# Moving 16 modulation tiles of a layer trunk into its one-hot gates stage, with two product banks there and per-pair counts in the HGRN stage

## The chip, the cores and the metric

One core of one Trainium2 chip. The metric is the device time of one execution in microseconds (us); a stretch "from A to B" is counted from the start of the profiled span.

## What is computed

Two layers of a hybrid decoder trunk, for 256 prompt tokens and 8 x 4 sample tokens, model width 1024, all in float32. What matters here, cut from the reference:

```
mod = silu(c) @ w_ada + b_ada                 # c: 1 prompt row + 8 sample rows; w_ada: 1024 x 6144 a layer
sh1, sc1, gt1, sh2, sc2, gt2 = split(mod, 6)
h = rmsnorm(x, norm1) * (1 + sc1) + sh1       # before the input projection
oa = hgrn2(q, k, v, log_f, S0)                # per chunk: o = (q e^G) S + (masked q k decay) v
S  = S * e^Gl + (k e^(Gl - G))^T v            # the state that goes from chunk to chunk
x = x + gt1 * (mixer(h) @ w_out)
h = rmsnorm(x, norm2) * (1 + sc2) + sh2
x = x + gt2 * peer(h)                         # product-key experts: top 16 of 128 x 128 for 8 heads a token
```

`w_ada` is read as 48 tiles of 128 x 1024 a layer: six sections (the six names of the split) of eight tiles.

## The kernel before

**Stages.** `build` runs a loop over the two layers. In each, the blocks follow one another with a barrier of all engines between them: `project_block` (norm and input projection), `local_block` (RG-LRU and norms of the delta heads), `hgrn_block`, `delta_block`, `output_block`, `experts_block` (scores, top 16 and the first expert matrix), `gates_block` and `combine_block` (second expert matrix). All weights arrive as tiles of 512 KB; SyncE issues each load when the slot of a ring comes free (`ring`, three slots, and in the local and HGRN blocks `extra_ring`, four slots, in turn with it).

**The modulation tiles.** `SECTIONS` puts the two sections of the norm ahead of the input projection last, and they are those of the next layer, since that norm stands at a layer's start; `setup_block` computes the first layer's. A tile is one `ada_product` (line 509): four matmuls, each of 32 output rows by 256 columns, that add into the bank `ps_mod`. After eight tiles a section is complete: ScalarE copies the rows (`copy_rows`, line 532), TensorE turns them with two matmuls by the identity (`ada_turn`, line 517), and ScalarE copies the columns into `m.mod` (`copy_columns`, line 539). The next section may not start before that. In `local_block` 16 tiles and two turns run, in `hgrn_block` 32 tiles and four turns, put by hand between the block's own matmuls (`ada(first, end)` and `turn(n)` in its TensorE program). Bias and gain are applied in `delta_block` on VectorE (`add_bias`, `norm_gain`).

**`local_block` (line 846).** VectorE's chain ends with lines 971 and 972, which read the matmuls of line 903. Behind `turn(0)` TensorE has the second eight tiles and `turn(1)`, and ScalarE the two copies of that section.

**`hgrn_block` (line 975).** C = 8 positions a block, 32 blocks, two pairs of heads. VectorE makes for each distance d in 0 to 7 the products q*gate*key (`pairs`), TensorE sums them per head (`distance`, line 1116), VectorE multiplies by the values and adds (`values`, lines 1242 and 1243). GpSimd makes the decays (line 1095) and the decayed keys (`kt`, lines 1100 and 1102); `kt_ready` follows them, and TensorE waits for it before it transposes keys and values (lines 1138 and 1140), and only behind these comes `distance(2)`. ScalarE writes masked copies of the values (`mask_v`, line 1070) for four steps of eight blocks; two copies are held. A step's matmuls (line 1171) give the updates of eight blocks in `ps_outer`, and VectorE walks the state through the blocks, pair by pair (line 1270): 64 operations, each behind a wait for the one before (`link`, a `Chain`), also where the two pairs have nothing to do with each other. `read_states` (line 1150) reads the state of each block into `ps_sums`, after a whole step of the walk (`scan_ready`). The matmuls of the sample group (line 1195) come after the whole walk (`u_out` 8), then VectorE's lines 1279, 1280 and 1282.

**`gates_block` (line 2397).** 64 groups of four prompt tokens. For a group TensorE makes distances in `ps_d` (`spots`, line 2419), VectorE one-hot rows times gate weight (line 2472), GpSimd distances of the second key (line 2449), ScalarE a one-hot of these by Square and Relu (lines 2459 and 2461), TensorE four matmuls (line 2429) into one of four banks of `ps_g`, and VectorE multiplies the expert activations by them (line 2479). Each engine is held by counts: GpSimd and the one-hot rows of group q wait for the products of group q - 4 (`gate_ps`), the products of group q for both one-hots and for line 2479 of group q - 4. SyncE has nothing to do, and no DMA runs.

## Time and profile before

| | us |
|---|---|
| median of 3 runs | 2382.62 (2380.51 to 2385.88) |
| the profiled execution, its own time | 2376.54 |
| its span | 2374.7 |
| TensorE busy in the span | 2274.7 (96%) |
| VectorE | 1515.3 (64%) |
| ScalarE | 1264.8 (53%) |
| GpSimd | 1051.2 (44%) |

The profiled execution is 6.08 us under the median of the runs. "Busy" for TensorE takes in modelled ends of pipelined matmuls, so a busy TensorE isn't one at its peak. The mean granted TensorE clock is 0.968 of full speed.

### The profile page before, as it was taken

What the parts mean: (1) busy time and instruction counts of PE and PEld (TensorE: products, weight loads), DVE (VectorE), ACT (ScalarE), POOL (GpSimd) and SP (SyncE); (2) the same over time, 40 slices, a digit from 0 to 9 for tenths busy, and PEclk for the clock granted to TensorE, in tenths of its full rate; (3) what the DMA queues carried; (4) which work ended last, traced back from release to release, by engine and by line L of the source; (5) the groups of instructions that cost most, each with busy time, mean ns of one, the idle gap of its engine ahead of it and who ended that gap; (6) DMA issues with size and microseconds to landing.
All of it is one profiled execution on the core that took longest, in us unless ns stands there. A gap on an engine that the chain in (4) does not pass through costs nothing. (4 is left out here: it accounts for less than half of the span.)

```text
span 2374.7 us, 58407 instructions
## 1 busy us (share of the span) xinstructions
PE 2274.7 (96%) x20514; PEld 2085.6 (88%) x20514; DVE 1515.3 (64%) x3131; ACT 1264.8 (53%) x2431; POOL 1051.2 (44%) x960
## 2 busy tenths in 40 slices
PE   6978999999999999999999799999999999999998
PEld 4955869999998799999989367699999978999997
DVE  2747636963225968888656665299432278787885
ACT  2543315567557955555546322155665587555554
POOL 0001106884446746566300210088644475665661
PEclk7988999999999999999989789999999999999999
DMA  6466034556552079899544830455555512898992
GB/s 263 163 249 240 4 125 160 177 177 207 189 187 98 5 274 314 277 311 312 177 161 158 307 124 29 143 177 178 198 184 188 189 36 89 292 312 275 312 311 100
DMA packets 123806, 455.40 MB, mean 192 GB/s; under 512 B 13744, under 2 KB 14256, under 8 KB 122544
## 3 DMA queue, kind: packets, MB, share of 16 engines
q1 hardware_dynamic: 105264, 386.80, 45.7%
q0 software_dynamic: 18432, 67.12, 10.3%
q8 instruction: 72, 1.18, 0.2%
q14 instruction: 38, 0.31, 0.0%
HBM read 449.37 MB, written 4.49 MB: 191 GB/s over the span
## 5 line engine op out<-in xcount | busy, mean ns | idle before, releaser
L426 POOL TENSOR_TENSOR parts<-ring,parts 128x512 fp32r<-128x512 f32 x358 | 463.9, 1299 | 470.7 <-ACT parts L419 455.7
L419 ACT ACTIVATE parts<-ring 128x512 fp32r<-128x512 f32 x616 | 386.7, 631 | 359.5 <-PE ps_u L475 281.7
L471 PE MATMUL ps_u<-h_parts,parts 128*128 128x256 f32 x4096 | 563.6, 280 | 0.9 <-ACT parts L419 0.6
L2594 PE MATMUL ps_y<-act_parts,parts 128*128 128x256 f32 x4096 | 561.3, 279 | 0.0
L471 PEld LDWEIGHTS ps_u<-h_parts,parts 128*128 128x128 f32 x4096 | 514.6, 188 | 3.2 <-ACT parts L419 2.0
L2594 PEld LDWEIGHTS ps_y<-act_parts,parts 128*128 128x128 f32 x4096 | 513.6, 188 | 0.9 <-ACT parts L2534 0.7
L426 DVE TENSOR_TENSOR parts<-ring,parts 128x512 fp32r<-128x512 f32 x258 | 178.6, 695 | 382.1 <-ACT parts L419 359.3
L2643 POOL TENSOR_TENSOR act_parts<-big,act_parts 128x256 fp32r<-128x256 f32 x256 | 246.7, 964 | 302.2 <-ACT act_parts L2623 302.2
L475 PE MATMUL ps_u<-h_parts,parts 128*128 128x256 f32 x2048 | 322.8, 279 | 1.2 <-DVE parts L426 0.9
L2598 PE MATMUL ps_y<-act_parts,parts 128*128 128x256 f32 x2048 | 321.7, 279 | 0.0
L475 PEld LDWEIGHTS ps_u<-h_parts,parts 128*128 128x128 f32 x2048 | 275.4, 188 | 2.0 <-DVE parts L426 1.3
L2598 PEld LDWEIGHTS ps_y<-act_parts,parts 128*128 128x128 f32 x2048 | 274.8, 188 | 0.0
L2541 DVE TENSOR_TENSOR parts<-ring,parts 128x512 fp32r<-128x512 f32 x260 | 214.4, 846 | 74.6 <-ACT parts L2534 73.9
L2541 DVE TENSOR_TENSOR parts<-more_ring,parts 128x512 fp32r<-128x512 f32 x252 | 209.2, 850 | 73.0 <-ACT parts L2534 73.0
L2623 ACT ACTIVATE act_parts<-big 128x256 fp32r (+1 forms) x256 | 107.2, 419 | 219.8 <-PE ps_y L2598 213.7
L2534 ACT ACTIVATE parts<-ring 128x512 fp32r<-128x512 f32 x260 | 162.2, 625 | 49.4 <-PE ps_y L2598 49.4
L2534 ACT ACTIVATE parts<-more_ring 128x512 fp32r<-128x512 f32 x252 | 157.3, 624 | 45.3 <-PE ps_y L2598 45.3
L2429 PEld LDWEIGHTS ps_g<-onehot 128*128 128x128 f32 x1024 | 123.9, 191 | 40.6 <-issue 36.4
L2449 POOL TENSOR_TENSOR onehot<-keep,sel 128x512 f32<-128x512 f32 x128 | 132.7, 1039 | 36.7 <-PE ps_g L2429 27.6
L2429 PE MATMUL ps_g<-onehot 128*128 128x128 f32 x1024 | 144.5, 284 | 4.3 <-ACT onehot L2461 3.4
L471 PE MATMUL ps_z<-x_parts,parts 128*128 128x288 f32 x832 | 136.3, 305 | 1.6 <-ACT parts L419 1.6
L471 PEld LDWEIGHTS ps_z<-x_parts,parts 128*128 128x128 f32 x832 | 121.8, 196 | 2.0 <-ACT parts L419 2.0
(391 smaller groups left out, 2853.3 us busy)
## 6 DMA issues: line engine op xcount, KB each, us to landing
ring<-in_stream SPq DMA_DIRECT2D x522, 512.0 KB, 3.9
more_ring<-in_stream SPq DMA_DIRECT2D x126, 512.0 KB
extra_ring<-in_stream SPq DMA_DIRECT2D x48, 512.0 KB, 6.2
big<-in_stream SPq DMA_DIRECT2D x16, 512.0 KB, 11.6
out_state_out<-big SPq DMA_DIRECT2D x2, 1440.0 KB, 8.0
big<-in_state SPq DMA_DIRECT2D x2, 1280.0 KB, 11.3
big<-in_mixc SPq DMA_DIRECT2D x2, 1024.0 KB, 8.8
big<-in_spots SPq DMA_DIRECT2D x2, 1024.0 KB, 5.4
```

Of the source, the lines that this page charges most:

```text
L419: eng.activation(m.parts[:, q % PARTS, 0, :], half_tile(m, t, half), ACT.Copy).then_inc(s["hi_ready"], 1)
L426: eng.tensor_tensor(m.parts[:, q % PARTS, 1, :], half_tile(m, t, half), m.parts[:, q % PARTS, 0, :].bitcast(F32), ALU.subtract).then_inc(m ...
L471: pe.matmul(out, hi[:, k, :], hr[:, side, kk, 0:tokens], start=(kk + side == 0), stop=False)
L475: mm = pe.matmul(out, lo[:, k, :], hr[:, 0, kk, 0:tokens], start=False, stop=(kk == KD - 1))
L2429: mm = pe.matmul(ps_g[:, g % SETS, c, :], first[:, g % SETS, c, :], second[:, g % SETS, c, :], start=True, stop=True)
L2449: pool.tensor_tensor(second[:, g % SETS, :, :], spread(m.iota, 1, GROUP), spread(tokens_of(m.second_key, i, g), 2, P), ALU.subtract).then_ ...
L2534: act.activation(m.parts[:, q % PARTS, 0, :], tile[:, half * D // 2:(half + 1) * D // 2], ACT.Copy).then_inc(s["hi_ready"], 1)
L2541: v.tensor_tensor(m.parts[:, q % PARTS, 1, :], tile[:, half * D // 2:(half + 1) * D // 2], m.parts[:, q % PARTS, 0, :].bitcast(F32), ALU.s ...
L2594: pe.matmul(ps[:, half * KD // 2 + k, :], hi[:, k, :], act_parts[:, j % AHEAD, side, :], start=False, stop=False)
L2598: mm = pe.matmul(ps[:, half * KD // 2 + k, :], lo[:, k, :], act_parts[:, j % AHEAD, 0, :], start=False, stop=False)
L2623: act.activation(act_parts[:, j % AHEAD, 0, :], column(g, j), ACT.Copy).then_inc(s["act_hi"], 1)
L2643: pool.tensor_tensor(act_parts[:, j % AHEAD, 1, :], column(g, j), act_parts[:, j % AHEAD, 0, :].bitcast(F32), ALU.subtract).then_inc(s["ac ...
```

## The change

It takes the 16 tiles of the two last sections out of the local and HGRN blocks, of which each now has eight fewer (8 and 24; one turn and three). The gates block gets them: SyncE loads them into a ring of three slots of its own, TensorE runs one behind the products of groups 1, 4, 7, ... 22 and 33, 36, ... 54 and turns a section behind groups 26 and 58, ScalarE copies rows after its groups 23 and 55 and columns after 31 and 63, for which its one loop becomes four. `ps_d` has two banks in place of four, since `ps_next` needs one; `spots` runs two groups ahead in place of three; TensorE's loop over groups is written out. Bias and gain of these two sections go from the delta block into the combine block. In the HGRN block the state walk counts per pair (`after0`, `after1`) and each operation waits for its own pair's last one; `pairs` and `values` wait for the operations that they need; the samples' kept states are multiplied before the walk; the samples' matmuls run after three steps of the walk; TensorE's order is written anew. `parts` is allocated for the blocks that use it, to make room for the new ring.

```diff
-MODS_T = len(SECTIONS) * KD
-LOCAL_ADA = 16
+MODS_T = 4 * KD
+NEXT_T = len(SECTIONS) * KD - MODS_T
+LOCAL_ADA = 8
...
+T_NEXT = T_X + EXTRAS
+TILES = T_NEXT + NEXT_T
...
+    if i >= MODS_T:
+        return T_NEXT + i - MODS_T
...
             mm.then_inc(s["qk_spread"], 1)
             turn(0)
-            ada(KD, 2 * KD)
-            turn(1)
...
             copy_rows(act, m, s, rows, ps_mod, 0)
             copy_columns(act, m, s, ps_mod, 0, 1)
-            copy_rows(act, m, s, rows, ps_mod, 1)
-            copy_columns(act, m, s, ps_mod, 1, 2)
...
+            copy_rows(act, m, s, ada_rows, ps_mod, 1)
+            copy_columns(act, m, s, ps_mod, 1, 1)
...
-            copy_rows(act, m, s, ada_rows, ps_mod, 3)
-            copy_columns(act, m, s, ps_mod, 3, 2)
+            copy_rows(act, m, s, ada_rows, ps_mod, 2)
+            copy_columns(act, m, s, ps_mod, 2, 2)
             mask_v(2)
-            copy_rows(act, m, s, ada_rows, ps_mod, 4)
-            copy_columns(act, m, s, ps_mod, 4, 3)
             mask_v(3)
             mask_v(4)
-            act.wait_ge(s["scan_ready"], 4)
+            copy_rows(act, m, s, ada_rows, ps_mod, 3)
+            copy_columns(act, m, s, ps_mod, 3, 3)
+            for pair in range(A_PAIRS):
+                act.wait_ge(s[f"after{pair}"], BLOCKS)
             act.activation(m.states[:, 0:A_PAIRS, 0, :], after[:, :, BLOCKS - 1, :], ACT.Copy)
-            copy_rows(act, m, s, ada_rows, ps_mod, 5)
-            copy_columns(act, m, s, ps_mod, 5, 4)
...
-                        pe.wait_ge(s["cols_out"], i // KD - 2)
+                        pe.wait_ge(s["cols_out"], (i - LOCAL_ADA) // KD)
...
-            ada(16, 22)
+            ada(8, 14)
             distance(0)
             distance(1)
-            ada(22, 24)
+            ada(14, 16)
             turn(1)
-            ada(24, 26)
...
-                if d == 5:
+                if d == 6:
                     turn(2)
-                ada(*((26, 28), (28, 30), (30, 32), (32, 33), (33, 35), (35, 37))[d - 2])
+                ada(*((18, 20), (20, 21), (21, 22), (22, 24), (24, 25), (25, 26))[d - 2])
...
-                pe.wait_ge(s["scan_ready"], turn + 1)
-                for b in range(turn * TB // 2 + 1, min((turn + 1) * TB // 2 + 1, BLOCKS)):
+                for pair in range(A_PAIRS):
+                    pe.wait_ge(s[f"after{pair}"], HALF * (turn + 1))
+                for b in range(turn * HALF + 1, min((turn + 1) * HALF + 1, BLOCKS)):
...
+            def products(step):
                 pe.wait_ge(s["vm_ready"], step + 1)
                 for pair in range(A_PAIRS):
-                    n = 2 * step + pair
-                    if n >= 4:
-                        pe.wait_ge(s["u_out"], n - 3)
+                    if step >= 2:
+                        pe.wait_ge(s[f"after{pair}"], HALF * (step - 1))
                     for r in range(2):
...
                     mm.then_inc(s["u_ready"], 1)
-                if step == 1:
-                    turn(3)
-                    ada(40, 42)
-                if step == 0:
-                    pe.wait_ge(s["qt_ready"], 1)
-                    pe.wait_ge(s["values_done"], 1)
-                    for b in range(NB):
-                        for pair in range(A_PAIRS):
-                            for r in range(2):
-                                inter(pair, r, NP + NS * b, NS, m.state0[:, pair, b, :])
-                    ada(37, 40)
-                if step >= 2:
-                    read_states(step - 2)
-                    ada(38 + 2 * step, 40 + 2 * step)
-            ada(46, 48)
+
+            def sample_products():
+                pe.wait_ge(s["vm_ready"], 5)
+                for pair in range(A_PAIRS):
+                    pe.wait_ge(s[f"after{pair}"], HALF * 3)
+                    for r in range(2):
+                        rows = slice(r * HD, (r + 1) * HD)
+                        mm = pe.matmul(ps_outer[rows, pair, :], ktt[0:NB * NS, 2, pair, rows],
+                                       vm[0:NB * NS, 0, 2 * pair + r, :, :], start=True, stop=True)
+                    mm.then_inc(s["samples_u"], 1)
+
+            products(0)
+            products(1)
+            pe.wait_ge(s["qt_ready"], 1)
+            pe.wait_ge(s["values_done"], 1)
+            for b in range(NB):
+                for pair in range(A_PAIRS):
+                    for r in range(2):
+                        inter(pair, r, NP + NS * b, NS, m.state0[:, pair, b, :])
+            ada(26, 28)
+            products(2)
+            read_states(0)
+            products(3)
+            read_states(1)
+            ada(28, 32)
+            sample_products()
...
+            turn(3)
             mm = read_states(3)
             mm.then_inc(s["inter_ready"], 1)
-            turn(4)
...
+                dst = {k: compact((pair_s if k else pair_p)[:, d % 2, :], k, d) for k in kinds(d)}
+                if d == 0:
+                    for k in kinds(d):
+                        i = ve.tensor_tensor(dst[k], blocks(q, k, 0, length(k)), blocks(key, k, 0, length(k)), ALU.mult)
+                    i.then_inc(s["products_ready"], 1)
+                    return
+                decayed = {k: steps(ve.tensor_tensor(dst[k], blocks(q, k, d, length(k)), blocks(gate[d], k, d, length(k)),
+                                                     ALU.mult)) for k in kinds(d)}
+                for k in kinds(d):
+                    steps.wait(decayed[k])
+                    i = ve.tensor_tensor(dst[k], dst[k], blocks(key, k, 0, length(k) - d), ALU.mult)
...
+                    return
+                tmp, valued = {}, {}
+                for k in kinds(d):
+                    tmp[k] = compact(prod_s if k else prod_p, k, d)
+                    steps.wait(summed[k])
+                    valued[k] = steps(ve.tensor_tensor(tmp[k], a[k], blocks(v, k, 0, length(k) - d), ALU.mult))
+                for k in kinds(d):
+                    steps.wait(valued[k])
+                    summed[k] = steps(ve.tensor_tensor(blocks(o, k, d, length(k)), blocks(o, k, d, length(k)), tmp[k], ALU.add))
...
+            steps.wait(steps.n)
             ve.sem_inc(s["values_done"], 1)
+            ve.wait_ge(s["gates_ready"], 1)
+            for pair in range(A_PAIRS):
+                last = blocks(since, True, NS - 1, NS)[:, pair, :, :].broadcast_to([P, NB, HD])
+                kept = steps(ve.tensor_tensor(m.states[:, pair, 1:, :], m.state0[:, pair, :, :], last, ALU.mult))
...
+                            ve.wait_ge(s[f"after{pair}"], b)
...
-                        link(i)
-                ve.sem_inc(s["scan_ready"], 1)
-                ve.sem_inc(s["u_out"], 2)
-            ve.wait_ge(s["u_ready"], 9)
+                        i.then_inc(s[f"after{pair}"], 1)
+            steps.wait(kept)
             for pair in range(A_PAIRS):
+                ve.wait_ge(s["samples_u"], pair + 1)
...
-                link(ve.tensor_tensor(new, m.state0[:, pair, :, :], last, ALU.mult))
-                link(ve.tensor_tensor(new, new, ps_outer[:, pair, :].rearrange("p (b v) -> p b v", b=NB), ALU.add))
+                ve.tensor_tensor(new, new, ps_outer[:, pair, :].rearrange("p (b v) -> p b v", b=NB), ALU.add)
             ve.wait_ge(s["inter_ready"], 1)
-            link(ve.tensor_tensor(o[:, :, C:], o[:, :, C:], ps_sums[:, 0:A_PAIRS, C:NT], ALU.add))
+            last = steps(ve.tensor_tensor(o[:, :, C:], o[:, :, C:], ps_sums[:, 0:A_PAIRS, C:NT], ALU.add))
+            steps.wait(last)
...
-                            add_bias(link, m, 0, 6 * KD, m.par("b_ada"))
+                            add_bias(link, m, 2 * KD, 6 * KD, m.par("b_ada")[:, 2 * KD:])
                         elif lv == 4:
-                            norm_gain(link, m, 0)
                             norm_gain(link, m, 1)
...
+    BANKS = 2
+    MOD_RING = 3
+    MOD_AT = [1 + 3 * n for n in range(KD)] + [33 + 3 * n for n in range(KD)]
+    MOD_TURNS = (26, 58)
+    names = ("spots_ready first_ready distance_ready square_ready second_ready gate_ps weighted mod_loaded0 mod_loaded1 "
+             "mod_loaded2 mod_done0 mod_done1 mod_done2 rows_out cols_ready cols_out")
+    with signals(nc, m, names) as s, \
             nc.sbuf_tensor("onehot", [P, 2, SETS, GROUP, P], F32) as onehot, \
-            nc.psum_tensor("ps_d", [P, SETS, GROUP, P], F32) as ps_d, \
+            nc.sbuf_tensor("mod_ring", [P, MOD_RING, D], F32) as mod_ring, \
+            nc.psum_tensor("ps_d", [P, BANKS, GROUP, P], F32) as ps_d, \
+            nc.psum_tensor("ps_next", [P, 512], F32) as ps_next, \
             nc.psum_tensor("ps_g", [P, SETS, GROUP, P], F32) as ps_g, nc.Block() as block:
...
+        @block.sync
+        def _(sp):
+            for n in range(NEXT_T):
+                if n >= MOD_RING:
+                    sp.wait_ge(s[f"mod_done{n % MOD_RING}"], n // MOD_RING)
+                sp.dma_start(mod_tile(n), stream[l, T_NEXT + n, :, :]).then_inc(s[f"mod_loaded{n % MOD_RING}"], 16)
...
+            def spots(q):
+                pe.wait_ge(s["first_ready"], q + 1 + SETS - BANKS)
+                i, g = q // STEP, q % STEP
...
+            def gates(q):
+                pe.wait_ge(s["weighted"], q + 1)
+                pe.wait_ge(s["first_ready"], q + 1 + SETS)
+                pe.wait_ge(s["second_ready"], q + 1)
...
-            for g in range(SETS - 1):
-                spots(0, g)
-            with pe.Fori(0, TURNS - 1) as i:
-                for g in range(STEP):
-                    spots(i, g + SETS - 1)
-                    gates(i, g)
-            for g in range(STEP):
-                if g + SETS - 1 < STEP:
-                    spots(TURNS - 1, g + SETS - 1)
-                gates(TURNS - 1, g)
+            def modulation(n):
+                if n == KD:
+                    pe.wait_ge(s["cols_out"], 1)
+                pe.wait_ge(s[f"mod_loaded{n % MOD_RING}"], 16 * (n // MOD_RING + 1))
+                ada_product(pe, m, n % KD, mod_tile(n), ps_next).then_inc(s[f"mod_done{n % MOD_RING}"], 1)
+
+            for q in range(BANKS):
+                spots(q)
+            for q in range(GROUPS):
+                if q + BANKS < GROUPS:
+                    spots(q + BANKS)
+                gates(q)
+                if q in MOD_AT:
+                    modulation(MOD_AT.index(q))
+                elif q in MOD_TURNS:
+                    n = MOD_TURNS.index(q)
+                    pe.wait_ge(s["rows_out"], n + 1)
+                    ada_turn(pe, m, ps_next, mod_rows).then_inc(s["cols_ready"], 1)
...
+            onehots(0, 3)
+            next_rows(0)
+            onehots(3, 4)
+            next_columns(0)
+            onehots(4, 7)
+            next_rows(1)
+            onehots(7, TURNS)
+            next_columns(1)
...
-                v.scalar_tensor_tensor(first[:, g % SETS, :, :], ps_d[:, g % SETS, :, :], 0.0,
+                v.scalar_tensor_tensor(first[:, g % SETS, :, :], ps_d[:, g % BANKS, :, :], 0.0,
...
+            scale, shift = m.mod[:, KD:2 * KD, :], m.mod[:, 0:KD, :]
+            biased = steps(v.tensor_tensor(scale, scale, spread(m.par("b_ada")[:, KD:2 * KD], 2, 1 + NB), ALU.add))
+            v.tensor_tensor(shift, shift, spread(m.par("b_ada")[:, 0:KD], 2, 1 + NB), ALU.add)
+            steps.wait(biased)
+            v.scalar_tensor_tensor(m.gain[:, 0, :, :], scale, 1.0, spread(m.par("norm1"), 2, 1 + NB), ALU.add, ALU.mult)
...
+@contextmanager
+def weight_parts(nc, m, name):
+
+    with nc.sbuf_tensor(name, [P, PARTS, 2, D // 2], F32R) as m.parts:
+        yield
...
-            gates_block(nc, m, l)
-            combine_block(nc, m, l, stream, u_rows)
+            gates_block(nc, m, l, stream)
+            with weight_parts(nc, m, "v_parts"):
+                combine_block(nc, m, l, stream, u_rows)
```

Host code fills the stream by `ada_index`, so the same tiles lie elsewhere in it.

## Rows read from the trace of the kernel before

**Rows 1.** The page's busy time, share of the span and instructions of each engine.

```profile
PE 2274.7 (96%) x20514; PEld 2085.6 (88%) x20514; DVE 1515.3 (64%) x3131; ACT 1264.8 (53%) x2431; POOL 1051.2 (44%) x960
```

**Rows 2.** Windows of core 0: the local and the gates stage of the first layer.

```profile
138.90:170.00 31.10, 23.82 (x172) 12.85 (x172) 12.71 (x15) 11.73 (x21) 1.10 (x7) 0.78 0.75 265
...
743.60:828.90 85.30, 82.03 (x576) 63.40 (x576) 81.13 (x128) 79.60 (x128) 66.36 (x64) 1.00 0.00 0
```

**Rows 3.** Timeline, ends of the local stage, both layers (start us, us, engine, line).

```profile
162.33 1.05 DVE L972 TENSOR_TENSOR big<-big,ps_q 128x864 f32<-128x864 f32 x1
...
169.54 0.24 ACT L543 ACTIVATE mod<-ps_mod 128x72 f32<-128x72 f32 x1 [0.72 <-PE ps_mod L522]
...
1328.05 1.05 DVE L972 TENSOR_TENSOR big<-big,ps_q 128x864 f32<-128x864 f32 x1
...
1336.03 0.23 ACT L543 ACTIVATE mod<-ps_mod 128x72 f32<-128x72 f32 x1 [0.72 <-PE ps_mod L522]
```

**Rows 4.** Timeline of the HGRN stage, first layer, up to distance(2).

```profile
170.08 0.16 DVE L1206 TENSOR_TENSOR big<-small 128x2 f32<-128x2 f32 x1 [6.70 <-remote]
...
180.69 0.95 DVE L1239 TENSOR_TENSOR big<-ps_sums,big 128x512 f32<-128x512 f32 x2 [1.78 <-PE ps_sums L1116]
...
186.69 0.69 PE L1138 MATMUL ps_outer<-keep,big 128*128 128x128 f32 x2 [1.54 <-POOLq L1104]
...
189.31 1.75 PE L1116 MATMUL ps_sums<-big 128*128 128x384 f32 x4
```

**Rows 5.** Windows of core 0: a stretch of the HGRN stage behind the transposes' start.

```profile
186.70:192.70 6.00, 6.00 (x32) 3.93 (x32) 5.05 (x14) 4.43 (x13) 1.44 (x1) 0.51 0.54 206
```

**Rows 6.** Timeline of the HGRN stage, first layer, from the state walk on.

```profile
198.98 0.64 PE L512 MATMUL ps_mod<-extra_ring,cond 128*32 128x256 f32 x8
199.43 0.61 PE L512 MATMUL ps_mod<-ring,cond 128*32 128x256 f32 x8
...
202.37 1.94 PE L1171 MATMUL ps_outer<-big 128*64 128x512 f32 x8
204.24 2.03 PE L1150 MATMUL ps_sums<-big 64*64 64x4 f32 x64
...
225.50 2.57 PE L1195 MATMUL ps_outer<-big 32*64 32x512 f32 x8 [1.48 <-DVEq L1274]
228.00 3.16 PE L1150 MATMUL ps_sums<-big 64*64 64x8 f32 x56
...
204.35 0.48 DVE L1268 COPY big<-ps_outer 128x64 f32<-128x64 f32 x2 [3.25 <-PE ps_outer L1171]
...
214.90 5.03 DVE L1270 SCALAR_TENSOR_TENSOR big<-big,ps_outer 128x64 f32<-128x64 f32 x16 [0.25 <-DVE big L1270]
...
231.28 0.74 DVE L1282 TENSOR_TENSOR big<-big,ps_sums 128x560 f32<-128x560 f32 x1 [0.31 <-PE ps_sums L1150]
...
210.30 6.48 ACT L1070 ACTIVATE big<-big 128x256 f32<-128x256 f32 x16
```

**Rows 7.** Timeline of the gates stage, first layer, its start.

```profile
743.63 1.02 PE L2419 MATMUL ps_d<-big 128*128 128x512 bf16 x4 [0.88 <-DVEq L2465]
...
747.64 1.13 PE L2429 MATMUL ps_g<-onehot 128*128 128x128 f32 x8
748.61 0.38 PE L2419 MATMUL ps_d<-big 128*128 128x512 bf16 x1
748.92 1.13 PE L2429 MATMUL ps_g<-onehot 128*128 128x128 f32 x8
...
748.05 0.72 ACT L2461 ACTIVATE onehot<-onehot,keep 128x512 f32<-128x512 f32 x1
...
744.04 1.89 DVE L2472 SCALAR_TENSOR_TENSOR onehot<-ps_d,sel 128x512 f32<-128x512 f32 x3 [4.02 <-PE ps_d L2419]
...
751.50 1.04 POOL L2449 TENSOR_TENSOR onehot<-keep,sel 128x512 f32<-128x512 f32 x1 [0.23 <-PE ps_g L2429]
```

**Rows 8.** The page's DMA issues: target, engine, count, KB, us to landing.

```profile
extra_ring<-in_stream SPq DMA_DIRECT2D x48, 512.0 KB, 6.2
```

115 lines of the change are left out of this document (50 added, 65 removed).

## The prediction, made before the changed kernel was run

> **What bounds the kernel now.** I read the page first, then the windows of the stages, then the timeline of the three that the change touches. TensorE is busy in 96% of the span [rows 1], so a gain must come from stretches in which it isn't at full work. The windows show two kinds of stage: in the local stage of 31.1 us the granted clock is 0.78 of full and DMA 0.75 busy, while in the gates stage the clock is 1.00, no byte moves, and TensorE, VectorE and ScalarE are all busy over 93% of the time [rows 2]. So the 16 tiles leave stages with gaps and enter one in which three engines run level; the question is which of the three has room.
>
> The local stage's own work ends with VectorE at 163.38 (162.33 + 1.05); the stage ends with the modulation's column copy at 169.78. In the second layer these are 1329.10 and 1336.26 [rows 3]. The HGRN stage starts at 170.08 and ends for VectorE at 232.02 [rows 4, 6]. I call times in it h + t, with h = 170.08; its end is h + 61.9.
>
> **Local stage.** Removed: eight tiles, a turn, two ScalarE copies, eight loads. Nothing else stands behind VectorE's last operation, and the first section's column copy is over before it. Gain 6.4 us in the first layer (169.78 - 163.38) and 7.2 in the second: 13.6.
>
> **HGRN stage up to distance(2).** Eight tiles fewer, and those that remain at the start were loaded during the local stage. VectorE's wait of 1.78 us for the first sums goes [rows 4]. But this gains nothing yet: TensorE waits for GpSimd's decayed keys until h + 16.6 (186.69), then transposes until h + 19.2 and does distance(2) until h + 21.0 [rows 4]. GpSimd's chain isn't touched, so the values of distance 2 start at h + 20.5 to 21.0 as before. Gain 0.
>
> **From there to the walk.** Before, the walk starts at h + 34.3 after an idle 3.25 us [rows 6]. VectorE has 24 operations of distances 2 to 7 in about 10 us; some 15 of them now need not wait for the one before. What that is worth is seen in the gates stage: three operations without a wait take 1.89 us, so they start 0.60 apart [rows 7], against 0.69 busy plus the few hundredths of a wait; I take 0.12 us each, 1.8 in all. TensorE's order then sets the step matmuls: distance(6), the turn (its rows wait for ScalarE's first 16 masked copies, which end at h + 26.6, since 16 take 6.5 us [rows 6] and the transposes that they need end at h + 19.2 to 20.1), a tile, distance(7), a tile. That puts the first step's matmuls at h + 29.4 and their end, 1.9 later [rows 6], at h + 31.3. VectorE has by then done the kept states, two operations that stood behind the walk. Gain so far 3.0.
>
> **The walk and the end.** Before, 16 operations of the walk take 5.03 us [rows 6], 0.31 each. Of two pairs in turn each waits only for the one before last; by the same 0.12 less an operation takes 0.20, a step 3.2. Then VectorE is no longer the bound, nor is ScalarE (8 masked copies in 3.3 us a step, ready before TensorE comes to them). TensorE is, from h + 29.4: four steps and the samples' matmuls, 5 x 1.87 (202.37 to 204.24) = 9.4; the samples' reads and four `read_states`, 5 x 2.0 = 10.0; six tiles at 0.45 (198.98 to 199.43) = 2.7; a turn, 0.5 [rows 6]. Together 22.6: h + 52.0, and VectorE's last operation 0.74 with 0.2 ahead of it: h + 52.9. Against h + 61.9 that is 9.0 us. From this I take 0.2 us for waits that the sum doesn't see: 8.8 a layer, 17.6 in all. Bounds: the granted clock is 0.51 in the 6 us from the transposes on [rows 5]. If the now longer idle time at the stage's start makes the transposes run at that lower level (1.2 GHz in place of 2.4), their 2.6 us double; the tail's sum of 22.6 us could hold a slow piece too, as the samples' matmuls (2.57) and last reads (3.16) have now [rows 6]. Lower end 5 us a layer. Upper end 10.5, if the chain to h + 29.4 closes up by 1.5 us.
>
> Of the walk the Trainium skill says something else, in "VectorE: DVE Perf Modes", section "The DRAIN you can't avoid": eight copies took the same time with a semaphore after each as with one after the last, and one should save operations, not semaphores. By that rule a step of the walk would stay at 5.03 us, which is the second rival below. The trace speaks against the rule: 0.60 between starts of operations that are each 0.69 busy [rows 7].
>
> **Gates stage.** The start of a group's products follows the end of ScalarE's Relu: 748.05 + 0.72 = 748.77, products at 748.92, and 747.64 to 748.92 is a period of 1.28 us [rows 7]. ScalarE never rests, so it sets the pace, and what it gets is paid in full: two row copies (0.38 each) and one column copy (0.24, the other is behind its last group). Each row copy also waits for a tile that TensorE starts behind the products of group 22 or 54, while ScalarE is only one group further: products 0.97, tile 0.45, its pipeline 0.2 against 1.28 gives a wait of 0.4 to 0.5. Sum for ScalarE: 2 x (0.38 + 0.45) + 0.24 = 1.9 us a layer. Its loop is cut in four; 64 groups at 1.28 are 81.9 of the stage's 85.3 us, so the loop's turns cost little now. No row shows an entry into a further loop; I add 0.2 for the three and leave 1 us each to the upper bound.
>
> TensorE: of the 1.28 us the products take 0.97 (747.64 to 748.61), and 0.31 go to the 512-column matmul of `spots` with the wait for ScalarE in it [rows 7]. 16 tiles of 0.45 and two turns of 0.5 are 8.2 us a layer. If nothing in the 0.31 is a wait, all of it is paid, above what ScalarE's own copies cost. If the 512 columns need only 0.21, as four of them start that far apart at the stage's start ((1.02 - 0.38) / 3) [rows 7], each group gives back 0.1, three groups 0.3 of a tile's 0.45, and the long stretch between groups 22 and 33 the rest. GpSimd shows how far TensorE may lag: the products of group 3 end at 751.32, GpSimd makes group 7 from 751.50 to 752.54 [rows 7], and ScalarE, at 1.28 a group, needs it at 753.8; so a lag up to 1.2 us costs ScalarE nothing. With 0.15 us of lag a tile it reaches 1.2 at the eighth, where ScalarE waits anyway. I take 2.5 us a layer, 5.0 in all; bounds 1.5 and 9.
>
> The first tile is asked for at the stage's start; by the page a load like it lands after 6.2 us [rows 8], group 1's products end some 5 us in. TensorE would wait about a microsecond, inside the same 1.2. Two banks: `spots` of group q + 2 needs the one-hot rows of group q, which VectorE has made two groups earlier. Covered by VectorE's order; if that cover went, see the last rival. GpSimd gets nothing; SyncE had nothing to do and has nothing behind its 16 loads.
>
> **The rest.** The delta block loses a third of a bias add and one gain operation, the combine block gets three operations of about 0.25 us on VectorE between two tiles, where TensorE is fed from three half-tile buffers. Taken as 0; if the cover is gone, 0.7 us a layer.
>
> **Sum.** -13.6 - 17.6 + 5.0 = -26.2 us. Against the profiled execution's own 2376.54 us that gives 2350.3; the median of the runs is 6.1 above that, and I carry the difference over: 2382.6 - 26.2 = 2356.4.
>
> **Rivals.**
> - *TensorE is full in the gates stage.* Every tile is paid: 8.2 + 0.6 for ScalarE's part, near 9 us a layer. For it: TensorE's rows stand end to end. Against it: products start 0.15 us behind every Relu, as of one who waits. Time 2356.4 + 13 = 2369. Chance 0.15.
> - *HGRN gives half.* The walk stays at 0.31 an operation, or the clock is low in the transposes. The walk then ends at h + 31.4 + 20.5 = h + 51.9, with reads and the last operation behind it h + 54.9, 2 us later than forecast; a low clock adds 2.6. Together 4.6 a layer: 2365. For it: the clock rows; against it: TensorE has fewer waits for DMA at the start. Chance 0.2.
> - *Nothing gained.* HGRN's end was held by something that the sum doesn't see, so only the local stage gives, and the gates stage takes it back: within 4.8 us of before, 2382. Chance 0.04.
> - *Slower: the two banks close a ring.* `spots` of group q + 4 stands on TensorE ahead of the products of q + 2 and waits for the one-hot rows of q + 2, which VectorE makes behind line 2479 of group q - 1, which waits for the products of q - 1. That ring of three groups costs 0.15 + 0.60 + 0.69 + 0.1 + 0.31 + 0.97 = 2.8 us, with a tile 3.3, against 3 x 1.28 = 3.84, so it is open. Were a wait of over 0.6 us in it, it would set the pace; slower than before begins where a group takes 1.28 + 31.2 / 128 = 1.52 us, at a ring of 4.6. At 1.6 us a group: 2382.6 - 31.2 + 41 = 2392. Chance 0.04.
>
> **How the numbers follow.** The forecast has 0.57, 2356.4. The range takes in both HGRN's upper end and the first two rivals: 2347 to 2369. About 0.2% (4.8 us) is what a measurement of this kernel can tell from no change. Faster: 0.92, from the forecast and the first two rivals; within: 0.04; slower: 0.04.
>
> **What would show it.** In the changed profile the local stage ends within 0.5 us of line 972's operation; the distances still wait for `kt_ready` near h + 16.6; the walk's steps take 3.2 us for 16 and start near h + 31; the sample matmuls come ahead of the walk's end; HGRN ends near h + 53. In the gates stage the period stays 1.28 between tiles, ScalarE shows two gaps of about half a microsecond behind groups 23 and 55, and the stage takes 87.8 us in place of 85.3. A stage of over 92 us, or a walk of 5 us a step, would make it wrong.

## The result, and the profile of the changed kernel

The changed kernel takes 2405.49 us (median of 4 runs, 2398.1 to 2415.6) against 2381.8 (2380.51 to 2385.88) for the kernel before on the same chip: a ratio of 1.0103, 95% interval [1.0085, 1.0121]. It is slower by 1%, where 2356.4 and faster by 1.1% was forecast. The profiled execution took 2399.88 us, its span 2398.1.

The page's busy line of the changed kernel, which answers to [rows 1]:

```profile
PE 2295.1 (96%) x20514; PEld 2128.0 (89%) x20514; DVE 1502.6 (63%) x3135; ACT 1267.6 (53%) x2431; POOL 1047.4 (44%) x960
```

TensorE has the same 20514 matmuls as before and is busy 20.4 us longer; its weight loads take 42.4 us more. No matmul was added, so they became slower. The stages, each from the first start of one group of instructions to that of the next, first and second layer:

| stage | from, to | before | after | forecast of both layers | measured |
|---|---|---|---|---|---|
| local | last `ps_z` matmul to VectorE's scaling of q | 36.0, 37.8 | 30.6, 31.1 | -13.6 | -12.1 |
| HGRN | to VectorE's last operation | 57.7, 58.0 | 49.6, 51.6 | -17.6 | -14.5 |
| delta, output, scores | to the first `ps_u` matmul | 144.4, 144.9 | 144.6, 147.3 | 0 | +2.6 |
| first expert matrix | to the first `ps_d` matmul | 367.9, 368.5 | 376.5, 376.5 | 0 | +16.6 |
| gates | to the first `ps_y` matmul | 85.7, 85.6 | 91.6, 91.6 | +5.0 | +11.9 |
| combine | to the last `ps_y` matmul | 362.0, 362.0 | 372.1, 372.1 | 0 | +20.2 |

With 1.3 us less in what stands outside this table, that is the 23.4 us between the spans. Local and HGRN do nearly what was worked out, and gates costs over twice its price. The loss of 36.8 us lies in two stages whose instructions the change doesn't edit.

Timeline of the changed kernel, the local stage's end and the HGRN stage of the first layer (start us, us, engine, line), which answers to [rows 3, 4, 6]:

```profile
161.72 1.05 DVE L972 TENSOR_TENSOR big<-big,ps_q 128x864 f32<-128x864 f32 x1
163.53 0.16 DVE L1207 TENSOR_TENSOR big<-small 128x2 f32<-128x2 f32 x1 [0.76 <-DVE big L972]
...
181.13 0.69 PE L1138 MATMUL ps_outer<-keep,big 128*128 128x128 f32 x2 [4.81 <-POOLq L1104]
...
202.47 3.16 DVE L1292 SCALAR_TENSOR_TENSOR big<-big,ps_outer 128x64 f32<-128x64 f32 x16 [0.45 <-PE ps_outer L1169]
...
210.02 1.94 PE L1179 MATMUL ps_outer<-big 32*64 32x512 f32 x8
...
214.41 2.16 PE L1150 MATMUL ps_sums<-big 64*64 64x8 f32 x56
...
216.62 0.74 DVE L1301 TENSOR_TENSOR big<-big,ps_sums 128x560 f32<-128x560 f32 x1 [3.92 <-PE ps_sums L1150]
```

The local stage ends with line 972's operation. With h = 163.53 TensorE still waits for the decayed keys until h + 17.6 (forecast 16.6), 16 operations of the walk take 3.16 us (3.2), and HGRN ends at h + 53.8 (52.9). In the second layer, with h = 1339.85, it ends only at h + 55.9. A row of the timeline there and a window of TensorE (its length, busy time with the number of matmuls, granted clock, DMA share, GB/s) show why:

```profile
1391.83 3.16 PE L1150 MATMUL ps_sums<-big 64*64 64x8 f32 x56
```

```profile
1388.80:1395.00 6.20, 6.19 (x118) 0.58 0.13 51
```

The last reads of the states take 3.16 us in place of the first layer's 2.16, at a mean granted clock of 0.58: most of this tail runs at the lower level, 1.2 GHz. The kernel before had the same 3.16 us in its first layer [rows 6].

The page's groups of the first expert matrix, of the kernel before and then of the changed one (busy us, mean ns of one | idle before):

```profile
L471 PE MATMUL ps_u<-h_parts,parts 128*128 128x256 f32 x4096 | 563.6, 280 | 0.9 <-ACT parts L419 0.6
L471 PEld LDWEIGHTS ps_u<-h_parts,parts 128*128 128x128 f32 x4096 | 514.6, 188 | 3.2 <-ACT parts L419 2.0
```

```profile
L473 PE MATMUL ps_u<-h_parts,u_parts 128*128 128x256 f32 x4096 | 576.3, 283 | 0.6 <-ACT u_parts L421 0.4
L473 PEld LDWEIGHTS ps_u<-h_parts,u_parts 128*128 128x128 f32 x4096 | 528.1, 192 | 2.7 <-ACT u_parts L421 1.4
```

Nothing waits more than before; each weight load takes 192 ns in place of 188. The spread (shortest, median and longest of a group, in ns) is seen in the weight loads between 600 and 640 us, before and then after:

```profile
L471 PEld LDWEIGHTS ps_u<-h_parts,parts x230: 187/188/189, 599.9 to 639.7; 128*128 128x128 f32 x115
L473 PEld LDWEIGHTS ps_u<-h_parts,u_parts x223: 192/192/192, 599.9 to 639.5; 128*128 128x128 f32 x112
```

Windows of TensorE in the first expert matrix and in the combine stage show the rate (the number behind x counts the matmuls that overlap the window, the next one is the granted clock, then the DMA share and GB/s), before and then after:

```profile
600.00:640.00 40.00, 40.00 (x345) 1.00 0.55 186
1100.00:1140.00 40.00, 40.00 (x345) 1.00 0.93 312
```

```profile
600.00:640.00 40.00, 40.00 (x336) 1.00 0.54 182
1100.00:1140.00 40.00, 40.00 (x335) 1.00 0.93 303
```

The clock is full in both, DMA is not busier, and there are 336 matmuls where there were 345. From one start to the next the trace of the kernel before has 113 to 120 ns in this window, 117 on average; that of the changed kernel has 120 every time. Both stages together have 12288 such matmuls, so 3 ns each make the 36.8 us. The input projection, with 288 columns, keeps its pace: from the first to the last start of a `ps_z` matmul it takes 102.0 and 101.6 us before, 101.3 and 101.4 after. What did change for these matmuls is where their operands lie. Before, `parts` (the stationary operand) began at byte 38016 of a partition and `h_parts` or `act_parts` (the moving one) at 210592. Now `u_parts` and `v_parts` begin at 198304, and the moving operands still at 210592. (These addresses are the kernels' own allocation; the profile doesn't show them.)

In the gates stage of the changed kernel, first layer, a timeline of three groups and a tile, and two rows of its waits (us in total, times, longest), beside [rows 7]:

```profile
745.02 1.05 PE L2466 MATMUL ps_g<-onehot 128*128 128x128 f32 x8
...
746.13 1.05 PE L2466 MATMUL ps_g<-onehot 128*128 128x128 f32 x8
...
747.23 1.05 PE L2466 MATMUL ps_g<-onehot 128*128 128x128 f32 x8
...
748.22 0.64 PE L516 MATMUL ps_next<-mod_ring,cond 128*32 128x256 f32 x8
...
748.79 0.39 PE L2458 MATMUL ps_d<-big 128*128 128x512 bf16 x1
749.01 1.05 PE L2466 MATMUL ps_g<-onehot 128*128 128x128 f32 x8
```

```profile
PEld ps_d L2458 <- DVE onehot L2537: 7.2, 16, 1.1
...
ACT sel L2512 <- PE ps_next L516: 3.3, 2, 1.7
```

Here a group takes TensorE 1.11 us, with a tile 1.78; three groups with a tile are 3.99 us where ScalarE's period of 1.28 would give 3.83. ScalarE waits 3.3 us for the two row copies, where 0.4 to 0.5 each was forecast. The wait of the weight load for the one-hot rows, 0.45 us at each tile, lies mostly beside the tile's own matmuls.

What a layer pays is seen best in ScalarE, which set the period before. In both layers 53 of its 63 steps from one Relu (line 2507) to the next are as long as before, 1.27 or 1.28 us. The other ten are longer, by 6.0 us together: two with a row copy by 2.03 each, one between groups 5 and 6 by 0.75, six at tiles by 0.17 each, and one with a column copy by 0.12. Three rows follow of the first row copy, then a window of TensorE ahead of the long step at the start, and the first tile in it:

```profile
770.52 0.72 ACT L2507 ACTIVATE onehot<-onehot,keep 128x512 f32<-128x512 f32 x1
772.90 0.38 ACT L2512 ACTIVATE sel<-ps_next 128x256 f32<-128x256 f32 x1 [1.66 <-PE ps_next L516]
...
773.83 0.72 ACT L2507 ACTIVATE onehot<-onehot,keep 128x512 f32<-128x512 f32 x1
```

```profile
741.50:744.80 3.30, 3.30 (x20) 0.51 0.52 185
```

```profile
743.79 1.07 PE L516 MATMUL ps_next<-mod_ring,cond 128*32 128x256 f32 x8
```

TensorE runs at 1.2 GHz there and the tile takes 1.07 us in place of 0.64. The 0.75 us go with this clock. In all 24 layers of the kernels with tiles in the gates stage, the steps of groups 4 to 6 are longer by nothing where TensorE has its full clock at the stage's start (six layers), by 0.6 to 0.8 us where it is at the lower level for about 3.4 us (ten), and by 2.0 where it is for about 6.8 (eight).

### The profile page after: what moved, and what is told of

Same layout as the page of the kernel before. It is cut to its first block and busy times, and to the rows that moved or that the text cites. A ratio compares the mean times of both kernels' runs of the same rounds, so it can differ in the third digit from the quotient of the medians.

```text
span 2398.1 us, 57939 instructions
## 1 busy us (share of the span) xinstructions
PE 2295.1 (96%) x20514; PEld 2128.0 (89%) x20514; DVE 1502.6 (63%) x3135; ACT 1267.6 (53%) x2431; POOL 1047.4 (44%) x960
## 5 line engine op out<-in xcount | busy, mean ns | idle before, releaser
L428 POOL TENSOR_TENSOR u_parts<-ring,u_parts 128x512 fp32r<-128x512 f32 x358 | 465.9, 1303 | 486.6 <-ACT u_parts L421 466.9
L473 PE MATMUL ps_u<-h_parts,u_parts 128*128 128x256 f32 x4096 | 576.3, 283 | 0.6 <-ACT u_parts L421 0.4
L2659 PE MATMUL ps_y<-act_parts,v_parts 128*128 128x256 f32 x4096 | 575.3, 283 | 0.0
L473 PEld LDWEIGHTS ps_u<-h_parts,u_parts 128*128 128x128 f32 x4096 | 528.1, 192 | 2.7 <-ACT u_parts L421 1.4
L2659 PEld LDWEIGHTS ps_y<-act_parts,v_parts 128*128 128x128 f32 x4096 | 528.3, 192 | 0.7 <-ACT v_parts L2599 0.7
L421 ACT ACTIVATE u_parts<-ring 128x512 fp32r<-128x512 f32 x512 | 322.0, 632 | 302.2 <-PE ps_u L477 299.1
L477 PE MATMUL ps_u<-h_parts,u_parts 128*128 128x256 f32 x2048 | 329.4, 283 | 0.3
L2663 PE MATMUL ps_y<-act_parts,v_parts 128*128 128x256 f32 x2048 | 329.2, 283 | 0.0
L477 PEld LDWEIGHTS ps_u<-h_parts,u_parts 128*128 128x128 f32 x2048 | 282.6, 192 | 0.7 <-POOL u_parts L428 0.7
L2663 PEld LDWEIGHTS ps_y<-act_parts,v_parts 128*128 128x128 f32 x2048 | 282.6, 192 | 0.0
L2606 DVE TENSOR_TENSOR v_parts<-ring,v_parts 128x512 fp32r<-128x512 f32 x260 | 211.4, 835 | 83.5 <-ACT v_parts L2599 82.4
L2606 DVE TENSOR_TENSOR v_parts<-more_ring,v_parts 128x512 fp32r<-128x512 f32 x252 | 206.5, 839 | 83.3 <-ACT v_parts L2599 83.0
L2599 ACT ACTIVATE v_parts<-ring 128x512 fp32r<-128x512 f32 x260 | 162.3, 626 | 54.2 <-PE ps_y L2663 54.2
L2599 ACT ACTIVATE v_parts<-more_ring 128x512 fp32r<-128x512 f32 x252 | 157.5, 625 | 50.1 <-PE ps_y L2663 50.1
L2466 PEld LDWEIGHTS ps_g<-onehot 128*128 128x128 f32 x1024 | 133.9, 194 | 17.0 <-issue 13.6
```

The costliest lines, as they stand in the source:

```text
L421: eng.activation(m.parts[:, q % PARTS, 0, :], half_tile(m, t, half), ACT.Copy).then_inc(s["hi_ready"], 1)
L428: eng.tensor_tensor(m.parts[:, q % PARTS, 1, :], half_tile(m, t, half), m.parts[:, q % PARTS, 0, :].bitcast(F32), ALU.subtract).then_inc(m ...
L473: pe.matmul(out, hi[:, k, :], hr[:, side, kk, 0:tokens], start=(kk + side == 0), stop=False)
L477: mm = pe.matmul(out, lo[:, k, :], hr[:, 0, kk, 0:tokens], start=False, stop=(kk == KD - 1))
L2466: mm = pe.matmul(ps_g[:, q % SETS, c, :], first[:, q % SETS, c, :], second[:, q % SETS, c, :], start=True, stop=True)
L2599: act.activation(m.parts[:, q % PARTS, 0, :], tile[:, half * D // 2:(half + 1) * D // 2], ACT.Copy).then_inc(s["hi_ready"], 1)
```

## Experiments on the operands' place

All times below are medians beside the kernel before, which stood at 2379.0, 2380.1, 2379.8 and 2379.0 us in the four sets of runs. "Changed" is the kernel after the change. The first set makes a cross: weight halves (stationary) and moving operands each on or off a multiple of 64 bytes.

**e1, weight halves moved by 32 bytes**, and the moving operands behind them by 64, so that these stay 32 off a multiple of 64. Edit of the changed kernel:

```diff
-    with nc.sbuf_tensor(name, [P, PARTS, 2, D // 2], F32R) as m.parts:
+    with nc.sbuf_tensor(name, [P, PARTS, 2, D // 2], F32R, align_bytes=64) as m.parts, \
+            nc.sbuf_tensor(f"{name}_pad", [P, 8], F32):
```

> The kernel after the change, with the weight halves (in_parts, u_parts, v_parts: the stationary operands) begun on a multiple of 64 bytes in SBUF, at 198336 in place of 198304; h_parts, x_parts and act_parts (the moving operands) stay 32 bytes off such a multiple. Theory A (the weight load of a float32 half tile is slower when it begins 32 bytes off a multiple of 64): the pace of a half tile in the expert matmuls and in the combine stage returns from 1.44 to 1.40 us, about 18.5 us a layer, so about 2405.5 - 37 = 2368, range 2362 to 2375. Rival B (it is the place: parts now lies beside the moving operands, behind the large array, in place of ahead of it): no change, 2398 to 2410. Rival C (the moving operand, or something else of the new layout, is what slowed): no change, 2398 to 2410.

Measured: 2370.12 us, ratio 0.9961 [0.9948, 0.9974].

**e2, moving operands moved by 32 bytes.** The same pad of 8 floats behind the weight halves, without `align_bytes`.

> The kernel after the change, with only the moving operands (x_parts, h_parts, act_parts, and more_ring with them) begun on a multiple of 64 bytes, by 32 bytes of padding behind the weight halves, which stay 32 bytes off. Theory A: no change, 2398 to 2410, half tiles at 1.44 us. Rival C (the moving operand's alignment decides): 2368 or below. Rival B: no change.

Measured: 2369.38 us, 0.9954 [0.9936, 0.9973]. Moving the other operand helps as much, which theory A excludes.

**e3, the kernel before with `parts` moved by 32 bytes**, and what lies behind it by 64.

```diff
+        sb("pad_ahead", [P, 8])
         self.parts = sb("parts", [P, PARTS, 2, D // 2], F32R)
+        sb("pad_behind", [P, 8])
```

> The kernel before the change, with 32 bytes of padding ahead of parts and 32 behind it, so that parts alone begins 32 bytes off a multiple of 64 and everything behind it keeps its place in a line of 64. Nothing else of the change is in it. Theory A: the half tiles of the expert matmuls and of the combine stage go from 1.40 to 1.44 us, so 2382 + 37 = 2419, range 2412 to 2426. Rival B (the region of SBUF): no change, 2378 to 2387.

Measured: 2388.53 us, 1.0036 [1.0021, 1.0051]: between the two expectations.

**e4, both moved by 32 bytes**: `align_bytes=64` and no pad.

> The kernel after the change with both the weight halves and the moving operands on multiples of 64 bytes. Theory A: as with the weight halves alone, about 2368. If the moving operand counts as well, below that run by more than 3 us. Rivals B and C as before: B no change, 2398 to 2410.

Measured: 2404.83 us, 1.0111 [1.008, 1.0142]: the whole loss is back. So neither operand's own place in a line of 64 bytes decides (A and C fall). What sorts the kernels is the distance between the two: 12288 bytes is slow, 12320 is fast. The next run tests that on the kernel before.

**e5, the kernel before at a distance of 163840 bytes.** `parts` is allocated behind `rms`; nothing else moves that these matmuls read.

```diff
         self.ring = sb("ring", [P, RING, D])
-        self.parts = sb("parts", [P, PARTS, 2, D // 2], F32R)
...
         self.rms = sb("rms", [P, NT])
+        self.parts = sb("parts", [P, PARTS, 2, D // 2], F32R)
```

> The four runs so far give a cross: weight halves and moving operands both 32 bytes off a multiple of 64 is slow (2405), one of the two moved by 32 bytes is fast (2370, 2369), both on multiples is slow again (2405). So theory R (for relative): what counts is the offset between the stationary and the moving operand. It is 12288 bytes in the slow kernels, 12320 in the fast ones, 172576 (32 over a multiple of 512) in the kernel before. Here the kernel before has parts allocated behind rms: the offset becomes 163840, a multiple of 4096, with parts still far from the moving operands and ahead of the large array. Theory R: half tiles at 1.44 us, 2379 + 35 = 2414, range 2408 to 2420. Rival B (it takes an offset of 12288, so neighbours at a multiple of 512, or a common region): no change, 2375 to 2386. Rival P (parts itself must be on a multiple of 64, as in the kernel before): its penalty was 9 us when tried alone, so about 2388.

Measured: 2417.22 us, 1.0156 [1.0142, 1.017]. That is the whole loss (37 us) in a kernel that has nothing of the change, so the place in the memory (rival B) falls too, and so does rival P, which expected 2388. Its windows have the changed kernel's rate:

```profile
600.00:640.00 40.00, 40.00 (x336) 1.00 0.53 184
1100.00:1140.00 40.00, 40.00 (x336) 1.00 0.91 303
```

**e9, e10, e15, other distances**: the changed kernel with pads of 16, 64 and 32 floats (here e9's).

```diff
-    with nc.sbuf_tensor(name, [P, PARTS, 2, D // 2], F32R) as m.parts:
+    with nc.sbuf_tensor(name, [P, PARTS, 2, D // 2], F32R) as m.parts, \
+            nc.sbuf_tensor(f"{name}_pad", [P, 16], F32):
```

> The kernel after the change with 64 bytes of padding between the weight halves and the moving operands: their offset is 12352, 64 over a multiple of 512. Offset 0 was slow by 35 us (three kernels), 32 fast (two and the kernel before), and the kernel before with parts moved to an offset 64 over a multiple of 512 was slow by 9. Theory R (the offset alone decides, wherever the two lie): about a quarter of the loss, 2369 + 9 = 2378, range 2374 to 2383. Rival (that kernel's 9 us came from parts itself being off a multiple of 64 there): 2369, range 2365 to 2373.

> As e9 with 256 bytes: offset 12544, 256 over a multiple of 512. Theory R with a collision that fades with distance: fast, 2369, range 2365 to 2373, half tiles of 12 matmuls at 1.40 us. Rival R2 (it repeats every 128 or 256 bytes): slow, 2400 to 2408. Rival R3 (farther is faster still): half tiles below 1.40 us and a time below 2362.

> The changed kernel with 128 bytes of padding between the weight halves and the moving operands: offset 12416, 128 over a multiple of 256. Offsets 0 and 256 were slow (2405, 2399), 32 and 64 fast (2369, 2369). Theory: it repeats every 128 bytes, so slow, 2398 to 2408. Rival: it repeats every 256, so fast, 2365 to 2373.

Measured: 2369.03 us (0.9961 [0.9943, 0.9979]), 2398.93 (1.0086 [1.0058, 1.0115]) and 2387.2 (1.0031 [1.0014, 1.0047]). In one table, by the distance modulo 512 bytes:

| distance mod 512 | kernels | median us | matmuls in 600:640 |
|---|---|---|---|
| 0 | changed, e4, e5 | 2405, 2405, 2417 | 336, 336, 336 |
| 32 | before, e1, e2 | 2379, 2370, 2369 | 345, 345, 345 |
| 64 | e3, e9 | 2389, 2369 | 342, 342 |
| 128 | e15 | 2387 | 339 |
| 256 | e10 | 2399 | 336 |

Within the changed kernel's family, and within that of the kernel before (before, e3, e5), the rate in the window orders the kernels nearly as their times do; e9 is the exception. A fade with distance doesn't fit: 256 is about as slow as 0, and 128 about half as slow. Both expectations of e15 missed, but a repeat every 256 bytes with a part of the loss at 128 fits all the distances tried, as one every 512 does; no run tells them apart. For 64 the expectation of 2378 missed in the changed kernel, and the time of its rival was hit. There the first expert matrix took 368.2 and 367.6 us, no more than before in spite of the 342; one combine stage took 358.9 us (less than the 362.0 before) and the other 365.3. In e3 the same stages took 371.4, 370.6 and twice 365.4. Why one distance gives two paces stays open.

One rival has no run: ScalarE, VectorE and GpSimd write the weight halves while TensorE reads, and their writes have the same distance to the moving operand. Against it, the changed kernel's weight loads all take 192 ns between 600 and 640 us, whichever of the three writes at the time; that doesn't exclude it.

## Experiments on the gates stage

All start from e2. **e6** has no tiles, turns, copies or loads in the gates stage.

```diff
-                sp.dma_start(mod_tile(n), stream[l, T_NEXT + n, :, :]).then_inc(s[f"mod_loaded{n % MOD_RING}"], 16)
...
-                if q in MOD_AT:
-                    modulation(MOD_AT.index(q))
...
-            next_rows(0)
...
-            next_columns(0)
```

> The kernel after the change with the moving operands moved by 32 bytes (2369 us, gates stage 91.7 us from its first distances to the first matmul of the combine stage, 85.7 before the change), without the 16 tiles, the turns, ScalarE's copies and the loads in the gates stage; so the two modulation sections are left out of the result. The two banks, the loop written out on TensorE and ScalarE's loop in four pieces stay. Theory T (tiles and copies cost it all; a group takes ScalarE 1.276 us and TensorE 1.11, so two banks cost nothing): the stage takes 85.4 to 86.2 us, the kernel about 12 us less than 2369, 2357. Rival K (the two banks or the cut loop cost): the stage stays above 88 us, and the kernel above 2362.

Measured: 2356.36 us, 0.9892 [0.9873, 0.991]; the stage takes 85.8 and 85.5 us, as before the change (85.7, 85.6). The result lacks the two modulation sections, so this run is only a measurement. Without tiles, two banks, the written-out loop and the cut loop of ScalarE cost nothing; the tiles with their copies cost all of the 6 us a layer.

**e7, row copies two groups later**, by two more pieces of ScalarE's loop.

```diff
-    MOD_TURNS = (26, 58)
+    MOD_TURNS = (28, 60)
...
-            next_rows(0)
-            onehots(3, 4)
+            onehots(3, 4, 2)
+            next_rows(0)
+            onehots(3, 4, STEP, 2)
```

> As the fast kernel of 2369 us, with ScalarE's row copies two groups later (behind its groups 25 and 57) and TensorE's turns behind groups 28 and 60. In the trace ScalarE waits 1.65 us for each row copy, since TensorE lags by then. Theory: ScalarE's 3.3 us a layer of waiting go, the stage takes 88.4 us, the kernel 2363, range 2361 to 2365. Rival (TensorE's lag is work that must be made up anyway, so the wait only moves to ScalarE's next groups): under 1 us a layer, 2367 to 2370.

Measured: 2367.67 us, 0.9934 [0.9913, 0.9955]. The stage takes 89.7 and 88.4 us, 2.0 and 3.2 less than in e2, and the waits no longer list line 2512. The second layer has the same low clock at its start as e2's layers (3.4 us of it) and gains the 3.3 that were forecast; the first has 6.8 us of it, which takes 1.25 back. So the theory holds in the stage, but the time of 2363 was missed and is too near to e2's to tell.

**e8, tiles spread evenly**, run again as **e14**.

```diff
-    MOD_AT = [1 + 3 * n for n in range(KD)] + [33 + 3 * n for n in range(KD)]
-    MOD_TURNS = (26, 58)
+    MOD_AT = [base + n for base in (0, 32) for n in (1, 4, 8, 11, 14, 18, 21, 24)]
+    MOD_TURNS = (30, 62)
```

> As the fast kernel of 2369 us, with the tiles spread evenly (behind groups 1, 4, 8, 11, 14, 18, 21, 24 of each half), row copies behind ScalarE's groups 27 and 59 and the turns behind TensorE's groups 30 and 62. With a tile every three groups the trace shows a cycle of 3.99 us where ScalarE alone would take 3.83: three groups of 1.11 us and 0.67 for a tile on TensorE. With seven groups to two tiles TensorE needs 7 x 1.11 + 2 x 0.67 = 9.11, ScalarE 8.93. Theory (TensorE is full): the stage takes 64 x 1.11 + 16 x 0.67 + 1 = 82.8 at the least, near 87 with its ends; the kernel 2360, range 2357 to 2364. Rival (the ring through GpSimd and ScalarE sets the cycle, not TensorE): a tile costs the same wherever it stands, and this equals the run with late rows, about 2363 to 2369.

> The kernel of the even tiles once more, beside the filled one and with more rounds: 2364.5 us before, so 2361 to 2368, and 0.992 of the kernel before, range 0.990 to 0.994.

Measured: 2364.49 us, 0.9921 [0.9903, 0.9938], and again 2360.76, 0.9919 [0.9896, 0.9942]. The stage takes 88.4 and 88.5 us in e8, 87.3 and 89.9 in e14, and 89.9 twice in e13 below, which has the same gates stage. Compared at the same clock at the start, this is e7 again: over the period of before, ScalarE's steps are longer by 2.9 us (e8, both layers) against 2.7 in e7, and by 4.1 or 4.2 (e14, e13) against 4.0. So in the stage e8's rival holds: spreading the tiles gives nothing beyond the late rows. Only e14's first layer, with full clock at its start, comes near the forecast 87. Both times lie just outside what was expected (up to 2364 for e8, from 2361 for e14).

## Experiments on HGRN and the clock

**e11, the kernel before with the walk's counts alone.**

```diff
+                            ve.wait_ge(s[f"after{pair}"], b)
                             i = ve.scalar_tensor_tensor(new, after[:, pair, b - 1, :],
...
-                        link(i)
+                        i.then_inc(s[f"after{pair}"], 1)
+                for pair in range(A_PAIRS):
+                    ve.wait_ge(s[f"after{pair}"], (turn + 1) * TB // 2)
```

> The kernel before with one part of the change alone: in the walk over the states each operation waits for its own pair's last one (after0, after1) in place of the last one of either pair. TensorE's order, the 48 tiles and everything else stay. In the changed kernel 16 operations took 3.16 us in place of 5.03. Theory (what was forecast: the wait costs, and 0.12 us of it an operation go): the walk's steps go to 3.2 us each; TensorE's own work from the first step's matmuls on (five sets of matmuls 9.4, reads 10, eleven tiles 5, two turns 1) is 25.4 against 31.5 us now, so HGRN ends 4 to 6 us earlier a layer: 2380 - 10 = 2370, range 2366 to 2374. Rival (a wait for a finished semaphore costs nothing, the gain of the walk in the changed kernel came from something else): 2380, steps at 5.0 us.

Measured: 2377.95 us, 0.9998 [0.9984, 1.0013]. Timeline of VectorE's walk in it, first layer:

```profile
203.51 2.76 DVE L1271 SCALAR_TENSOR_TENSOR big<-big,ps_outer 128x64 f32<-128x64 f32 x14
208.50 3.15 DVE L1271 SCALAR_TENSOR_TENSOR big<-big,ps_outer 128x64 f32<-128x64 f32 x16 [2.23 <-PE ps_outer L1171]
```

The steps fall to 3.15 us, so the price of the wait was right. VectorE then waits for TensorE between steps (2.23 us above), and HGRN gets shorter by 4.0 and 1.7 us. But the stages from there to the first expert matmul get longer, by 3.2 and 7.7 us, and the time stays what it was: the steps are as the theory has them, its 2370 is missed.

**e12, the walk chained again**, on e2.

```diff
                             ve.wait_ge(s[f"after{pair}"], b)
+                            ve.wait_ge(s[f"after{1 - pair}"], b + pair)
```

> The fast form of the changed kernel (2369 us, moving operands moved by 32 bytes) with the walk's counts undone: each operation waits for both pairs' last ones, so for the one before it. The rest of the change stays. Theory: 16 operations take 5.03 us again, VectorE ends the walk at 197.4 + 20.3 = 217.7 in place of 213.5, and the reads that follow make HGRN 3 us longer a layer: 2369 + 6 = 2375, range 2371 to 2379. Rival (the walk is no longer what ends last, TensorE's order is): within 2 us of 2369.

Measured: 2392.78 us, 1.0047 [1.0031, 1.0063], 23 us over e2. Its walk:

```profile
203.54 18.37 DVE L1293 SCALAR_TENSOR_TENSOR big<-big,ps_outer 128x64 f32<-128x64 f32 x48 [0.50 <-DVE big L1293]
...
209.35 3.68 PE L1169 MATMUL ps_outer<-big 128*64 128x512 f32 x8 [2.64 <-DVE big L1293]
```

48 operations in 18.37 us are 6.1 for 16, more than the 5.03 of [rows 6]. With two waits each, one of them on the other pair's count, they cost more than with one, so the run isn't a clean undoing. HGRN takes 63.5 and 63.7 us, 13.3 and 13.7 more than in e2, where 3 was expected. Both the theory's size and the rival fall: in the new order TensorE's products and reads wait for the walk, by 2.64 us in the second row, so each of its steps counts.

**The stretch behind HGRN.** Windows of TensorE from HGRN's end to the first expert matmul (the number behind the parenthesis is the mean granted clock), both layers, of the kernel before, then of e2:

```profile
232.00:375.70 143.70, 135.73 (x1772) 0.95 0.21 72
1398.80:1543.00 144.20, 136.03 (x1771) 0.95 0.21 71
```

```profile
219.10:364.20 145.10, 135.49 (x1771) 0.95 0.21 71
1379.20:1531.30 152.10, 142.59 (x1770) 0.90 0.20 68
```

The same 1771 matmuls take 152.1 us at a mean clock of 0.90 and 144.2 at 0.95; time by clock is 137 in both, so the clock accounts for the difference. Over the profiled executions this stretch, counted from the start of VectorE's last operation, takes 144.3 to 145.8 us in the kernels with the long HGRN stage (before, e3, e5, e12), all eight layers. With the shorter one (the changed kernel, e1, e2, e4, e6 to e11, e13 to e15) it takes from 144.6 to 152.8, and 147 or more in 19 of 26 layers. More of it is then at half clock. The length of the HGRN stage alone doesn't sort the layers, though: 56.1 us of it stand ahead of 144.3 in e5 and 56.3 ahead of 152.7 in e11, and 51.8 ahead of 144.7 in e1. So this is a count over one profile of each kernel; no run shows the cause.

**e13, TensorE's idle gap filled**, on e8: `keep_busy` (line 843) runs ten matmuls of 512 columns into a free bank.

```diff
             ada(16, 18)
+            keep_busy(pe, m, ps_outer[:, 3, :], 10)
             pe.wait_ge(s["kt_ready"], 1)
```

> The kernel of the even tiles (2364.5 us: offset 32, tiles spread evenly in the gates stage), with ten matmuls of 512 bf16 columns into a bank that is free there, ahead of TensorE's wait for GpSimd's decayed keys in the HGRN stage, where it stands idle for 4.8 us. Theory G (clock): after that gap the clock is granted at half for the 2.6 us of transposes, and a shorter HGRN stage leaves more half-clock time behind it in the delta and output stages (152.8 against 144.9 us there in half of the layers). Filled, the transposes run at full clock and the low stretches behind get shorter: 2 to 8 us less than the run without, 2357 to 2363. Rival (the fill does nothing: the clock is decided elsewhere): within 2 us of it, 2362 to 2367.

Measured: 2358.32 us, 0.9904 [0.9878, 0.9929], beside 0.9919 for e14 in the same set. That is in the theory's range and 2.4 us under e14, but the intervals overlap. The rows of the transposes tell more, in e14 and then in e13:

```profile
181.51 0.69 PE L1138 MATMUL ps_outer<-keep,big 128*128 128x128 f32 x2 [4.79 <-POOLq L1104]
182.00 0.63 PE L1140 MATMUL ps_outer<-keep,big 128*128 128x128 f32 x2
```

```profile
178.12 2.33 PE L847 MATMUL ps_outer<-keep 128*128 128x512 bf16 x10
182.13 0.44 PE L1139 MATMUL ps_outer<-keep,big 128*128 128x128 f32 x2 [1.68 <-POOLq L1104]
182.41 0.38 PE L1141 MATMUL ps_outer<-keep,big 128*128 128x128 f32 x2
```

Windows over the transposes, again of e14 and of e13:

```profile
181.40:184.20 2.80, 2.69 (x13) 0.50 0.01 4
```

```profile
182.10:184.00 1.90, 1.87 (x14) 1.00 0.03 11
```

They run at 1.2 GHz (0.50 of full) in e14 and at 2.4 in e13, after 4.8 us of idle time in the one and 2.3 us of matmuls and 1.7 of idle time in the other. HGRN takes 48.7 and 49.0 us against 49.9 and 50.0: the fill gives 1 us a layer. The stretch behind takes 147.5 and 152.7 us, in e14 147.4 and 147.2. So in this one profile (of an execution 7 us above e13's median) the fill gives nothing back there; that half of theory G isn't borne out, and what decides the clock there is open.

The transposes ran at the lower level in the kernel before as well. Windows over them, first layer, before and then after:

```profile
186.70:189.30 2.60, 2.60 (x12) 0.50 1.00 381
```

```profile
181.10:183.70 2.60, 2.57 (x12) 0.50 0.11 44
```

## Why the prediction was wrong, step by step

- **The step that failed** is the one that costs the rest at nothing: "Taken as 0" for everything outside the stages that the change edits. The move of `parts`, told in front as a matter of room, isn't in the sum at all. It put 12288 bytes between stationary and moving operand, and the matmuls of the two expert matrices went from 117 to 120 ns: 36.8 of the 49.6 us between forecast (2350.3 for the profiled execution) and profile. e2 takes 36 us back with 32 bytes, and e5 makes 37 us in the kernel before. The rivals had no such case either. All were mechanisms of the edited stages, and the slower one (two banks close a ring) finds no support in e6, where two banks without tiles cost nothing.
- **Local stage**: right, 12.1 for 13.6.
- **HGRN**: right in mechanism, 14.5 for 17.6. The walk's steps (3.16 for 3.2), TensorE's order and the wait for the keys came as worked out; the start of the transposes came 1 us later than taken. The second layer gains 1.7 us less than the first, as more of its tail ran at the lower clock, which the prediction named as a bound: its sum takes 2.0 us for the last reads, and they took 2.16 and 3.16. The other half of that bound and of the rival "HGRN gives half", a low clock that doubles the 2.6 us of the transposes, was a misreading. The clock of 0.51 in [rows 5] is that of the transposes themselves, so their 2.6 us were at the lower level already, and they are as long after the change. At full clock they would give 1 us a layer, as e13 shows.
- **Gates stage**: 11.9 for 5.0, or 5.9 a layer for 2.5; inside the bounds of 1.5 and 9, if they are a layer's, as the first rival's near 9 us a layer has them. The step that failed is the price of the row copies' waits. The sum has TensorE lag by 0.15 us a tile and calls a lag up to 1.2 us free; both came nearly so (three groups give back 3 x (1.28 - 1.11) = 0.51 of a tile's 0.67, which leaves 0.16, and only six tiles of 16 lengthen ScalarE's steps). But at the row copy, behind the eighth tile, ScalarE must wait out this lag: 0.45 was taken and 1.65 measured, about 8 x 0.16 + 0.45. With the copies that is 4.1 us a layer for 1.7; e7 took the waits away. The rest is 1.0 at six tiles and 0.75 from the low clock at the stage's start, which the sum didn't have. The first rival, every tile paid in full, did not come true.
- **The stretch behind HGRN** was taken as unchanged and is not: it lost 2.6 us in the changed kernel's profile and 9.3 in e2's. The clock accounts for it; why the clock is lower there is not shown.
- Without the misplaced operands (e2) the change gives 0.9954, about 10 us; by its own sum it should have given 26. In e2's profile, whose span is 7 us under the one before, 19 are missing: 7 in the gates stage, 9 in the stretch behind HGRN and 3 in the local and HGRN stages.

On the wait itself the Trainium skill's page "VectorE: DVE Perf Modes", section "Rules for kernel authors", advises to save operations rather than semaphores. The runs speak against that for these short operations: 5.03, 3.15 and 6.1 us for the same 16 operations with a wait for the last, a wait for the last but one, and both waits.

The version to keep is e13 (2358.32) or e8, whose repeat e14 took 2360.76 beside it: about 0.8 to 1% faster than the kernel before, and 2% faster than the changed one. The two can't be told apart.

## What to carry to other kernels

When a change moves a buffer, it edits every instruction that reads it: compare the addresses of matmul operands before and after, and the page's mean time of untouched matmuls first when a total surprises. A pad of 32 bytes between the stationary and the moving operand was worth more here than the whole change. A stage that wasn't edited can also run at another granted clock than before, so price a saving by the total and not by the stage. And where one engine may lag behind another for free, look for the point at which the other has to wait for it: the lag is paid there in one piece.

## What the chip showed that was not expected

- A matmul's pace depends on the distance between its two operands in SBUF: 345 matmuls in 40 us at 32 bytes over a multiple of 512, 339 at 128, 336 at 0 and at 256 (256 columns, float32, a weight load for each). The Trainium skill's page "SBUF — State Buffer", section "Who interferes with whom", gives TensorE two independent read ports, for the moving operand and for the weights, and says that it never waits on anyone. By that rule 32 bytes of padding would change nothing; measured, they give 36 us.
- An operation of VectorE behind two semaphore waits starts later than behind one, though one of the two had come an operation earlier: 0.38 us an operation in e12 against 0.31. The second wait is also on another count there, so which of the two costs isn't separated.
- One kernel's stretch from HGRN to the experts takes 145.8 us in one layer and 152.8 in the other (e2), by the clock that is granted in it. The longer case came up only in kernels with a shorter HGRN stage, but no run shows that this is the cause.
- At the start of the gates stage the same instructions cost ScalarE 0, 0.7 or 2.0 us, as TensorE is at 1.2 GHz there for none, 3.4 or 6.8 us.
